# Two attentions beside projections: the shapes of TensorE's array gathered into one visit a step, and the projections in halves of a unit

## The reference

```
z = einsum('bqhd,bshd->bhqs', qb, kb) * scale               # stick-breaking, a block of 128 rows against all keys before
log_keep = where(s < t, -softplus(z), 0)
tail = cumsum(log_keep, reverse=True) - log_keep
w = where(s < t, exp(log_sigmoid(z) + tail), 0);  o_sb = w @ v
...
q = apply_rope(rms_norm_2(q)); k = apply_rope(rms_norm_2(k))  # window attention, keys t-128 < s <= t, with a sink
probs = softmax(concat([scores, sink]))[..., :-1];  o_swa = probs @ v_band
...
merged = gates[0] * (o_sb @ w_branch_sb) + gates[1] * (o_swa @ w_branch_swa)
```

## Time and profile before

| what | us |
|---|---|
| median of 3 runs | 2659.11 (2658.48 to 2659.41) |
| profiled execution, its own time | 2658.53 |
| its span | 2657.0 |
| TensorE busy | 2625.0 (99%), VectorE 57%, ScalarE 43%, GpSimd 6% |
| the attentions, about | 1276 to 1466 and 1978 to 2168 |

### The profile page before, as it was taken

One profiled execution on the slowest core, in us unless ns is written; L12 is line 12 of the kernel. 1 busy time (PEld: TensorE's weight loads), 2 busy tenths in 40 slices (PEclk: granted clock), 3 DMA queues, 4 the chain that ended last, 5 costly groups with the idle time before them and its releaser, 6 DMA issues.

```text
span 2657.0 us, 32191 instructions
## 1 busy us (share of the span) xinstructions
PE 2625.0 (99%) x13046; PEld 2106.6 (79%) x13054; DVE 1514.9 (57%) x2100; ACT 1143.0 (43%) x1694; POOL 161.2 (6%) x147
## 2 busy tenths in 40 slices
PE   8999999999999999999999999999999999999998
PEld 6777778888887888888767888888877778888887
DVE  4566657474778665667765554433456754544433
ACT  6444344242467433335566334322346652423322
POOL 2222010000010000000111000000001100000000
PEclk9999999999999999999999999999999999999999
DMA  4111113222333323322211322223321123223332
GB/s 170 60 60 60 53 55 111 96 95 96 111 95 95 107 95 99 100 96 95 72 59 61 96 95 94 97 95 99 99 80 56 56 80 95 95 95 96 101 97 72
DMA packets 66674, 235.38 MB, mean 89 GB/s; under 512 B 7520, under 2 KB 8160, under 8 KB 66528
## 3 DMA queue, kind: packets, MB, share of 16 engines
q1 hardware_dynamic: 63504, 228.35, 26.7%
q10 hardware_dynamic: 3024, 4.99, 0.6%
HBM read 231.21 MB, written 2.10 MB: 88 GB/s over the span
## 4 chain that ended last, share of the span: by engine, by line
PE 89%; DVE 6%; ACT 3%; issue 2%; DMA 0%; POOL 0%; SPq 0%; ACTq 0%; DVEq 0%
PE bank L466 27%; PE bank L468 27%; PE bank L467 27%; DVE w_lo_k L1490 1%; PE bank L815 1%; PE bank L836 1%; ACT w_hi_k L985 1%; PE bank L885 1%; PE bank L825 1%; DVE xr_lru L1801 0%; PE bank L903 0%; PE bank L893 0%; DVE kept_att L1920 0%; PE bank L676 0%; DVE rot_att L1948 0%
## 5 line engine op out<-in xcount | busy, mean ns | idle before, releaser
L466 PE MATMUL bank<-x_hi_k,w_hi_k 128*128 128x512 f32 x2152 | 865.7, 402 | 12.1 <-DVE x_lo_k L1497 11.2
L468 PE MATMUL bank<-x_hi_k,w_lo_k 128*128 128x512 f32 x2152 | 840.6, 391 | 0.0
L985 ACT ACTIVATE w_hi_k<-raw_k 128x1024 fp32r<-128x1024 f32 x431 | 454.7, 1059 | 895.2 <-PE bank L468 893.6
L467 PE MATMUL bank<-x_lo_k,w_hi_k 128*128 128x512 f32 x2152 | 839.5, 390 | 0.0
L1490 DVE TENSOR_TENSOR w_lo_k<-raw_k,w_hi_k 128x1024 fp32r<-128x1024 f32 x431 | 534.7, 1241 | 166.2 <-ACT w_hi_k L985 165.7
L466 PEld LDWEIGHTS bank<-x_hi_k,w_hi_k 128*128 128x128 f32 x2152 | 404.7, 188 | 110.7 <-issue 14.6
L468 PEld LDWEIGHTS bank<-x_hi_k,w_lo_k 128*128 128x128 f32 x2152 | 404.6, 188 | 86.4
L467 PEld LDWEIGHTS bank<-x_lo_k,w_hi_k 128*128 128x128 f32 x2152 | 405.2, 188 | 82.1 <-issue 4.1
L466 PE MATMUL bank<-y_hi_k,w_hi_k 128*128 128x512 f32 x1136 | 445.6, 392 | 3.2 <-DVE y_lo_k L1836 1.9
L468 PE MATMUL bank<-y_hi_k,w_lo_k 128*128 128x512 f32 x1136 | 442.9, 390 | 0.0
L467 PE MATMUL bank<-y_lo_k,w_hi_k 128*128 128x512 f32 x1136 | 442.8, 390 | 0.0
(11 more groups left out here) (319 smaller groups left out, 2277.1 us busy)
## 6 DMA issues: line engine op xcount, KB each, us to landing
raw_k<-wstream SPq DMA_DIRECT2D x431, 512.0 KB, 3.5
outT<-h_k ACTq DMA_DIRECT2D x8, 256.0 KB, 2.8
h_k<-xT SPq DMA_DIRECT2D x4, 256.0 KB, 8.7
h_k<-xT ACTq DMA_DIRECT2D x4, 256.0 KB, 8.1
decay_mix<-constants ACTq DMA_DIRECT2D x4, 256.0 KB, 2.7
vec_k<-vectors SPq DMA_DIRECT2D x1, 282.5 KB, 10.3
cos_mix<-constants SPq DMA_DIRECT2D x1, 256.0 KB, 10.0
sin_mix<-constants SPq DMA_DIRECT2D x1, 256.0 KB, 10.2
```

The lines of the kernel that those rows point to most:

```text
L466: pe.matmul(dst, wh, rh, start=start, stop=False)
L467: pe.matmul(dst, wh, rl, start=False, stop=False)
L468: return pe.matmul(dst, wl, rh, start=False, stop=stop)
L985: act.activation(k.w_hi[:, u % SPLIT, :], k.raw[:, u % RAW, :], ACT.Copy).then_inc(*hi_done.mark())
```

## The change

In TensorE's program one generator, `pairs_in_step`, takes the place of `stick` and `window`. At slot 4 of each step it puts, without anything of the fill between: the window attention's masks, the logits' masks, the logits (now added onto the masks), the scores, the output of the step before, and the window attention's output. So a stick output comes 2 slots earlier than before. The turn of the probabilities comes at +4 instead of +6, and the window output at +6 instead of +9, on TensorE, ScalarE and (one slot later) VectorE. For part 0 three of four blocks a half are turned and copied, since its first block isn't read. The other engines keep `stick` and `window` as they are. The fill comes in 2 parts at a time (12 matmuls) on every engine, the lags in numbers of parts being halved.

```diff
+BESIDE = 2
...
+TURN_AT, OUT_AT = 4, 6
...
 def filling(fill, parts):
     for _ in range(parts - 1):
-        fill.part()
+        fill.part(BESIDE)
         yield
-    fill.part()
+    fill.part(BESIDE)
...
-SPLIT_LAG, EVICT_LAG, LOW_LAG = 1, 1, 4
+SPLIT_LAG, EVICT_LAG, LOW_LAG = 0.5, 0.5, 2
...
+        parts = len(fill.units) * PARTS // BESIDE
...
+        def logit_masks(g):
+            if g % TC == 0:
+                pe.wait_ge(*dve_done.at("qk", layer, g // TC))
+            if g > 0:
+                pe.wait_ge(*act_done.at("stick_wT", layer, g - 1, 1))
+            i = row_tile(g)
+            for half in range(2):
+                pe.matmul(ch(z_view(k, half, i), i), k.id_b[:], k.mask_b[:, 0:P], start=True, stop=False, skip_group_check=True)
...
-        def turned(m, part):
+        def local_turned(m, part):
             pe.wait_ge(*dve_done.at("probs", layer, m, part))
             for half in range(2):
-                for j in range(4):
+                for j in range(1 - part, 4):
...
+        for slot in range(WINDOW_SLOTS):
+            g, at = divmod(slot, STEP)
+            local = [(m, slot - PAIR_SLOTS * m) for m in range(PAIRS)]
+            scored = [(m, part) for m, t in local for part in range(2) if t == PART_AT[part]]
+            ended = [(m, part) for m, t in local for part in range(2) if t == PART_AT[part] + OUT_AT]
+            if at == 1 and 1 <= g <= ROWS:
+                turned(g - 1, 0)
+            if at == 2 and 1 <= g <= ROWS:
+                turned(g - 1, 1)
+            if at == 3 and g % TC == 0 and g < ROWS:
+                values(g // TC)
+            for m, t in local:
+                if t == norm_slot(m, SUMS_AT):
+                    local_sums(m)
+                for part in range(2):
+                    if t == PART_AT[part] + TURN_AT:
+                        local_turned(m, part)
+            if at == 4 and g <= ROWS:
+                for m, part in scored:
+                    local_masks(m, part)
+                if g < ROWS:
+                    logit_masks(g)
+                    logits(g)
+                for m, part in scored:
+                    local_scores(m, part)
+                if g > 0:
+                    output(g - 1)
+                for m, part in ended:
+                    local_output(m, part)
             yield
...
-        interleave(*layer_tasks(stick(layer), window(layer), (Fill(beside_pairs(layer), fill_piece), 0)))
+        steps = (pairs_in_step(layer), WINDOW_SLOTS, 0, 1)
+        interleave(steps, *beside_steps((Fill(beside_pairs(layer), fill_piece), 0)))
...
-                    if at == PART_AT[part] + 6:
+                    if at == PART_AT[part] + TURN_AT:
                         act.wait_ge(*pe_done.at("pT", layer, m, part))
                         for half in range(2):
-                            act.activation(k.pT[:, half, :], bank[6 + half][:], ACT.Copy).then_inc(*mark("pT", layer, m, part))
-                    if at == PART_AT[part] + 9:
+                            act.activation(k.pT[:, half, (1 - part) * P:], bank[6 + half][:, (1 - part) * P:],
+                                           ACT.Copy).then_inc(*mark("pT", layer, m, part))
+                    if at == PART_AT[part] + OUT_AT:
...
-                    if at == PART_AT[part] + 10:
+                    if at == PART_AT[part] + OUT_AT + 1:
```

More of the change, by code:

```diff
@@ L362, in filling, with beside_steps @@
     for _ in range(parts - 1):
[L363 removed]
+        fill.part(BESIDE)
         yield
[L365 to L368 removed]
+    fill.part(BESIDE)
+SPLIT_LAG, EVICT_LAG, LOW_LAG = 0.5, 0.5, 2
+def beside_steps(*fills):
+    tasks = []
+    for fill, lag in fills:
+        parts = len(fill.units) * PARTS // BESIDE
+        tasks.append((filling(fill, parts), parts, lag / parts, (parts + lag) / parts))
+    return tasks
 def layer_tasks(stick, window, *fills):
     tasks = [(stick, STICK_SLOTS, 0, STICK_SLOTS / WINDOW_SLOTS), (window, WINDOW_SLOTS, 0, 1)]
[L373 to L376, removed]
+    return tasks + beside_steps(*fills)
 def window_slots():
@@ L805, in values, with local_masks @@
             mm.then_inc(*mark("v_t", layer, pair))
-        def logits(g):
-            i = row_tile(g)
+        def local_masks(m, part):
+            if part == 0:
+                pe.wait_ge(*dve_done.at("wq", layer, m))
+            if part == 1 or m > 0:
+                pe.wait_ge(*dve_done.at("part_y", layer, m - 1 + part, 1 - part))
+            if part == 1 and m + 1 < PAIRS:
+                pe.wait_ge(*act_done.at("wq_mean", layer, m + 1))
+            if part == 0 and m == 0:
+                pe.wait_ge(*act_done.at("wq_mean", layer, 0))
+            masks = k.mask_b[:, 3 * P:5 * P].rearrange("p (o s) -> p o s", o=1).to_broadcast([P, 2, 2 * P])
+            for half in range(2):
+                pe.matmul(bank[6 + half][:], k.id_b[:], masks if part else k.mask_b[:, P:5 * P], start=True, stop=False,
+                          skip_group_check=True)
+        def logit_masks(g):
             if g % TC == 0:
@@ L812, in logits, with local_scores @@
                 pe.wait_ge(*act_done.at("stick_wT", layer, g - 1, 1))
+            i = row_tile(g)
+            for half in range(2):
+                pe.matmul(ch(z_view(k, half, i), i), k.id_b[:], k.mask_b[:, 0:P], start=True, stop=False, skip_group_check=True)
+        def logits(g):
+            i = row_tile(g)
             for half in range(2):
                 r = head_rows(half)
[L815 to L818, removed]
+                pe.matmul(z_view(k, half, i), k.aq[r, i * P:i * P + P], k.ak[r, 0:seen_keys(i)], start=False, stop=True,
+                          skip_group_check=True).then_inc(*mark("z", layer, g, half))
+        def local_scores(m, part):
+            for n in (2 * part, 2 * part + 1):
+                before = max(n - 1, 0) * P
+                to = (n % 2 + 1) * 2 * P
+                for half in range(2):
+                    r = head_rows(half)
+                    mm = pe.matmul(bank[6 + half][:, to - (n + 1) * P + before:to], k.wq[r, n * P:n * P + P], k.wk_t[r, before:(n + 1) * P],
+                                   start=False, stop=n % 2 == 1, skip_group_check=True)
+            mm.then_inc(*mark("scores", layer, m, part))
         def turned(g, half):
@@ L838, in output, with local_sums @@
             mm.then_inc(*mark("att_o", layer, g))
[L840 to L859, removed]
+        def local_sums(m):
             pe.wait_ge(*act_done.at("wq_sq", layer, m))
@@ L865, in sums, with local_output @@
             mm.then_inc(*mark("wq_sum", layer, m))
[L867 to L887, removed]
-        def turned(m, part):
+        def local_turned(m, part):
             pe.wait_ge(*dve_done.at("probs", layer, m, part))
             for half in range(2):
-                for j in range(4):
+                for j in range(1 - part, 4):
                     mm = pe.transpose(ch(bank[6 + half], j), ch(k.p_t[:, half], j), k.ident)
             mm.then_inc(*mark("pT", layer, m, part))
-        def output(m, part):
+        def local_output(m, part):
             n = 2 * part
```

12 lines of the change are left out of this document (1 added, 11 removed).

## The result

The change made the kernel slower: 2683.48 us (2683.16 to 2684.30) against 2658.80, a ratio of 1.0094 [1.0078, 1.0109]. A second set gave 2688.44 us (2686.95 to 2690.29), a ratio of 1.0109 [1.0092, 1.0126]. The forecast was 2666 us, with a range of 2650 to 2677. A fourth execution of the first set, the profiled one, had TensorE at 0.56 of its clock throughout and took 4374.20 us (with it the median of the four is 2683.89), so it is left out here, and the profile read is of an execution of the second set, 2689.72 us by its own time.

The account below looks back on a forecast made before the run. The prediction took TensorE's issue plus its waits as the bound: 26.8 us of added waits less 19.8 saved over two attentions gave +7.0 on a median of 2659.11, so 2666 us, range 2650 to 2677.

Parts of the forecast that it names:

- A granted clock under 1.00 there: Sign of being wrong: TensorE's granted clock below 1.00 in an attention; no size given.
- pair 0, 384 keys: Row tile 2 step, turn of probabilities after one block: need 8.4 us against 5.1 of TensorE work, wait 3.3.
- pair 1's seam: Pair 1, first to second step: local masks ahead of the logits wait for the turned queries, 1.3 us.
- pair 2's first step: At 512 keys, stick_w's halves turned together after one block: need 6.7 us against 4.5 from the logits, wait 2.2.
- pair 2's seam: Pair 2, second to third step: no block between turn and next masks, stick_wT behind a split and table load, 0.7 us.
- The four covers that were called long enough: Turns of probabilities in pair 1 both parts, pair 2 part 0, pair 3 part 1: cover 6.5 to 7.9 us, cost at most 0.1.
- The saving: TensorE issue per attention: 9.0 us from fewer shape visits (48 to 17) plus 0.9 from transposes, 9.9 together.
- inner change: Change from half rows to half columns inside 15 of 17 visits per attention, taken as 0.1 us each.
- rival 3: The change from half rows to half columns costs a whole visit, 0.34 us: 7.2 us more, 2673, slower; chance 0.12.
- Rivals 1 and 2: Waits at their floor: 2648, chance 0.18. Only the probabilities wait, 4.2 us at pair 1 and 2 absorbed: 2658, chance 0.25.
- Rival 4: The 0.35 us belongs to the return to products, not the shape; same saving as the forecast, no chance of its own.
- ceiling of 40 us: Upper bound on added waits in two attentions, half again 13.4 each, if scans and GpSimd collide at every step.

Follow-up runs that it names:

- turn at +5: The changed kernel with the turn of the probabilities 5 slots after the scores instead of 4, output still at 6: 2668.11 us, 1.0033.
- useless work: The changed kernel with 65 matmuls of no use per attention put ahead of eight of TensorE's waits: 2677.35 us, 1.0069.
- late kernel in blocks of 12: The changed kernel with the window attention's turn and output back at +6 and +9, the output its own visit, fill still 12 products: 2668.57 us, 1.0036.
- kernels that only gather: The changed kernel with window turn and output back at +6 and +9, fill in parts of 6: 2659.61 us; the same with two waits moved: 2654.08 us.
- early kernel in parts of 6: The changed kernel with the fill in parts of 6 products and the old lags, turn and output still at +4 and +6: 2674.46 us, 1.0061.
- blocks of 12 alone: The kernel before the change with the fill in parts of 12 products and the lags halved, nothing else: 2668.96 us, 1.0038.

## Why the prediction was wrong

Its direction was right, and so was what it gave as the reason: visits saved, cover lost. The time was 17.5 us too low (22.4 in the second set). Per attention it had 13.4 of waits less 9.9 saved, +3.5; measured were +14.9 and +16.4. Three terms were too kind. By the sum at the end of this section, the 25 us that the forecast lacked in the profiled execution are 9.7 of clock, 8.2 of waits and 6.8 of saving: the largest is one that it had put at nothing.

- **The step that failed: the clock.** The sum took TensorE at 1.00 throughout and added waits as if each cost its own length. "A granted clock under 1.00 there" stood among the signs of being wrong, but no case had a price for it. The clock fell behind the waits, 15.4 us of it in seven stretches, and filling the waits gave 6 to 11 us back. The Trainium skill ("TensorE: Matmul & The Clock Gate", Part 1) says that a clock gate takes TensorE from 2.4 to 1.2 GHz when it has lately been idle. The two levels agree with the rows. The prediction listed waits of up to 3.3 us and did not weigh this rule against them.
- **Waits in the places that were named: right.** As idle time in the first attention, forecast against measured: pair 0, 384 keys, 3.3 against 3.61 (1.97 + 1.64); pair 0, 128 keys, 2.3 against 2.19; pair 1's seam 1.3 against 1.38; pair 2's first step 2.2 against 2.84; pair 2's seam 0.7 against 0.32; pair 2, 128 keys, 3.1 against 2.87; pair 3, 384 keys, 2.6 against 2.40. The method, cover on TensorE against need elsewhere, row by row, held to 0.64 us each. The four covers that were called long enough cost 0.22 in one place and 0.09 in another. At pair 2's first step the forecast had scan and product at 1.6 each; measured were 1.22 and 1.99, and a rotation of 1.23 stood before the scan (0.69 in the kernel before).
- **Waits in sum: too small by 4 us per attention.** 20.7 against 16.5. Some 1.7 of it is the wait for land_v (1.57 + 0.16), which the grain of 12 makes alone; the prediction looked at the grain only as lost cover of the turns. The rest: the places named above agree as idle time, but were worked out as issue time, in which each of sixteen idle stretches is 0.16 us longer.
- **Who is waited for: half right.** The scalings of p_t were named for about 11 us in four waits. They ended 7.8 in five; in the 384-key steps GpSimd's stick_w, turned just before, took the first 1.97 and 1.54 us. The turn at +5 shows that the turn of p_t was nonetheless the thing to move: its waits vanish, and those for stick_w don't grow.
- **The saving: too large.** 9.9 forecast. Kernels with few half-clock stretches or none show 7.7 (turn at +5) and 6.6 (useless work). What it is made of, from interruptions alike but for one edit: logits and scores in one visit give 8 x 0.29 = 2.3; the stick output in it 15 x 0.2 = 3.0 (2.04 + 0.79 for the two apart at 128 keys, 2.63 for one); the window output 0.35 eight times, 2.8 (3.08 + 1.21 for the two apart in the late kernel in blocks of 12, 3.94 for one with the turn at +5, at 512 keys); transposes 0.9; masks ahead of logits -8 x 0.08 = -0.6, in the eight steps without scores, since the 0.29 has it for the others. That is 8.4, still above the measured 6.6 to 7.7; the rest was not traced. The failed terms are the masks' new place, which was priced at nothing, and the inner change.
- **The inner change of shape (rival 3).** It was taken as 0.1 us, with 0 and 0.34 as ends. A visit saved 0.2 of its 0.34 when the shape inside it changed, so the change costs about 0.14. TensorE's timeline, the changed kernel, a full visit at 512 keys:

```profile
1379.40 0.39 PE L475 MATMUL bank<-x_hi_k,w_lo_k 128*128 128x512 f32 x1
1379.63 0.29 PE L835 MATMUL bank<-mask_b_att,id_b_att 128*128 128x128 bf16 x2
1379.85 1.13 PE L841 MATMUL bank<-ak_att,q_att 64*128 64x512 f32 x4
1380.91 0.44 PE L870 MATMUL bank<-stick_wT_att,vt_att 128*64 128x128 f32 x4
1381.17 1.04 PE L896 MATMUL bank<-pT_att,wvt_att 128*64 128x256 f32 x12
1382.14 0.50 PE L473 MATMUL bank<-x_hi_k,w_hi_k 128*128 128x512 f32 x1
1382.48 0.40 PE L474 MATMUL bank<-x_lo_k,w_hi_k 128*128 128x512 f32 x1
```

  From 1379.40 to 1382.48 are 3.08, less two steps (0.46) is 2.62. By the prediction's prices the streams take 0.84 + 0.13 + 1.09 = 2.06, so 0.56 are left for a visit, where 0.44 was forecast. Those 0.56 are 0.34 for the visit, 0.14 for the inner change and 0.08 for the masks ahead. Rival 3 asks for 0.68 and falls. The Trainium skill ("TensorEngine Tiling (Array Packing)", Key Properties) has a drain at every change of mode; the rows show a cost at this one too, 0.14 us, less than half the 0.34 of going out to the full array and back.
- **Rivals 1 and 2** (waits at their floor; only the probabilities wait) fell: waits were above the forecast, and pair 1's seam and pair 2's first step had 1.38 and 2.84 us. **Rival 4** (the shape is not the cost) falls by the kernels that only gather: their work is 4.9 and 5.0 us less, of which 0.9 are the transposes.
- **The range.** The prediction had written a ceiling of 40 us for what the waits add in both attentions; measured were about 35. That ceiling alone, less the saving, was +20, or 2679, and the range was cut at 2677.

The sum as it should have been, for both attentions, the second estimated from the first: waits 2 x 17.5 = 35.0; work 2 x -6.5 = -13.0; products at half clock 4.0 in the first and 5.7 in the second (1.7, half of 3.4 us, for its one stretch more), 9.7 together: +31.7, against 31.2 measured in that execution.

## What to carry to other kernels

Price a wait that a change adds to TensorE at more than its length: two or three microseconds of idleness here brought stretches of 3.4 to 6.8 us at half clock, and a quarter to over a third of the loss was that. Gathering array shapes is worth 0.2 to 0.4 us a visit, but what it gathers must not be moved closer to what it waits for; keep the old distances first, look at which wait grew, and shift that one (here, with the wait for the queries moved too, 2659.61 us became 2654.08). And a coarser grain of filler work is not neutral: the blocks of 12 alone cost 10 us, because waits end where the filler can't be cut.

## What the runs showed of the hardware

- The clock falls behind waits under 3 us, but not behind each. In the changed kernel falls followed idle stretches of 1.97 + 1.64 us and of 2.19 and 2.87 in both attentions. Behind 2.84 us (before 1388.44) it stayed at 1.00 there, and fell behind the same wait in both attentions with the turn at +5. Behind 1.55 + 0.86 us it stayed in the first attention of the changed kernel (before 1450.47) and fell in the second (at 2168.4). The shortest that a fall followed: 0.59 + 1.64 us in the first attention of the early kernel in parts of 6, where 0.61 + 1.65 in the second brought none, and 1.93 us alone with the turn at +5, where 1.96 in the other attention brought none. Waits of up to 1.97 us in the late kernel in blocks of 12 brought none either. What decides it is open. So two executions of one kernel can differ: the mean granted clock was 0.996 to 0.997 in the first set and 0.993 to 0.994 in the second, some 8 us of clock, and the times were 2683.48 and 2688.44.
- Useless matmuls in the waits made the kernel 11.1 us faster than the second set without them (2688.44 to 2677.35), and 6.1 faster than the first.
- A causal mask added in front of the logits costs 0.08 us more than behind them, with the same instructions. Why is open: what the timelines show is only that the two masks then hold TensorE for 0.20 us instead of 0.13.
